# A mixture-of-experts block on one core: the last 128 tokens taken out of the dense expert products

## The reference, cut to what matters

```python
q = (xb @ w_q).reshape(p, 8, 2, 64)                    # 8 heads, two half queries
sc = einsum('phcd,hcnd->phcn', q, sub_keys)             # 128 scores for each half
top_s, top_i = top_k(sc, 16)
cand_s = top_s[:, :, 0, :, None] + top_s[:, :, 1, None, :]   # 16 x 16 sums
best_s, best_pos = top_k(cand_s.reshape(p, 8, 256), 16)
idx = take_along_axis(cand_i, best_pos, -1)             # first * 128 + second: one of 16384 experts
g = softmax(best_s)
act = gelu(einsum('phkd,pd->phk', expert_u[idx], xb))
out = einsum('phk,phkd->pd', g * act, expert_v[idx])    # 8 x 16 = 128 experts for each token
```

## Time and profile before

| | |
|---|---|
| time | 2292.05 us median of 3 runs (2291.0 to 2293.1) |
| span of the profiled execution | 2289.3 us |
| PE | 2225.7 us busy, 97% of the span |
| DVE, POOL, ACT | 1618.5, 1084.8 and 844.6 us busy (71%, 47%, 37%) |
| first product, 128 blocks | from 303.7 to 915 us of the span |
| second product, 128 blocks | from 922 to 1512 us |
| moved by DMA | 470.89 MB, 206 GB/s over the span |

### The profile page before, as it was taken

How to read it: one execution, slowest core, us unless ns; L and a number is a source line. 1 busy time by engine, 2 the same in 40 slices (tenths; PEclk the granted TensorE clock), 3 DMA queues, 4 the chain that set the end, 5 groups by cost and what they waited for, 6 DMA issues and landing times.

```text
span 2289.3 us, 30027 instructions
## 1 busy us (share of the span) xinstructions
PE 2225.7 (97%) x11272; PEld 2021.6 (88%) x11272; DVE 1618.5 (71%) x3044; ACT 844.6 (37%) x1317; POOL 1084.8 (47%) x695
## 2 busy tenths in 40 slices
PE   6999999999999999899999999999999999999998
PEld 3777889999999999899999999998877778888887
DVE  6774789998899763899898898747765565434323
ACT  4433433334333433333333333344355434323221
POOL 1334305878888787566566666354333331111100
PEclk9999999999999999899999999999999999999999
DMA  7647756668777885999999999633323333333332
GB/s 300 198 124 243 226 143 175 165 146 200 178 183 173 213 231 132 355 405 404 411 390 387 391 381 411 218 110 103 116 80 110 129 129 94 99 102 92 97 101 78
DMA packets 209848, 470.89 MB, mean 206 GB/s; under 512 B 50844, under 2 KB 106268, under 8 KB 208992
## 3 DMA queue, kind: packets, MB, share of 16 engines
q1 hardware_dynamic: 136552, 317.02, 42.3%
q0 software_dynamic: 73152, 151.94, 21.0%
HBM read 403.68 MB, written 61.28 MB: 203 GB/s over the span
## 4 chain that ended last, share of the span: by engine, by line
PE 58%; POOL 1%; DVE 1%; DMA 1%; issue 0%; ACT 0%; ACTq 0%
PE bank L571 15%; PE bank L572 15%; PE bank L575 15%; PE bank_stat L950 1%; PE bank_stat L951 1%; PE bank_stat L955 1%; PE bank_stat L572 1%; PE bank_stat L571 1%; PE bank_stat L575 1%; POOL expert_coefs L2533 1%; PE bank L995 1%; PE bank L982 1%; PE bank L980 1%; PE bank L723 1%; PE bank_stat L598 0%
## 5 line engine op out<-in xcount | busy, mean ns | idle before, releaser
L571 PE MATMUL bank<-h_lo,weights_hi 128*128 128x416 f32 (+1 forms) x2148 | 790.2, 368 | 8.4 <-DVE gates L2336 3.8
L572 PE MATMUL bank<-h_hi,weights_hi 128*128 128x416 f32 (+1 forms) x2148 | 788.4, 367 | 0.0
L1134 ACT ACTIVATE weights_hi<-weights_raw 128x1024 fp32r<-128x1024 f32 (+1 forms) x411 | 432.1, 1051 | 442.0 <-PE bank L575 318.4
L1658 DVE TENSOR_TENSOR weights_lo<-weights_raw,weights_hi 128x1024 fp32r<-128x1024 f32 x351 | 443.3, 1263 | 133.7 <-ACT weights_hi L1134 130.6
L2533 POOL DMA_INDIRECT expert_coefs<-square x256 | 447.8, 1749 | 156.0 <-issue 80.0
L575 PE MATMUL bank<-h_hi,weights_lo 128*128 128x416 f32 (+1 forms) x2148 | 479.6, 364 | 4.7 <-DVE weights_lo L1658 4.4
L571 PEld LDWEIGHTS bank<-h_lo,weights_hi 128*128 128x128 f32 x2148 | 407.8, 190 | 41.6 <-DVE gates L2336 3.9
L575 PEld LDWEIGHTS bank<-h_hi,weights_lo 128*128 128x128 f32 x2148 | 402.7, 188 | 37.5 <-DVE weights_lo L1658 7.1
L572 PEld LDWEIGHTS bank<-h_hi,weights_hi 128*128 128x128 f32 x2148 | 407.0, 189 | 31.0 <-issue 0.2
L2461 POOL TENSOR_TENSOR weights_lo<-weights_raw,weights_hi 128x1024 fp32r<-128x1024 f32 x60 | 147.0, 2455 | 222.6 <-ACT weights_hi L1134 222.6
L1345 ACT ACTIVATE hidden<-bank 128x416 f32<-128x416 f32 x128 | 66.3, 518 | 358.1 <-PE bank L575 336.5
(11 more groups left out here) (470 smaller groups left out, 3567.7 us busy)
## 6 DMA issues: line engine op xcount, KB each, us to landing
weights_raw<-in_expert_u SPq DMA_DIRECT2D x128, 512.0 KB
weights_raw<-in_expert_v SPq DMA_DIRECT2D x128, 512.0 KB
weight<-expert_coefs POOLq DMA_DIRECT2D x32, 832.0 KB
hidden_store<-hidden SPq DMA_DIRECT2D x28, 832.0 KB
hidden<-hidden_store POOLq DMA_DIRECT2D x28, 832.0 KB
ada_raw<-in_w_ada SPq DMA_DIRECT2D x34, 512.0 KB, 6.3
expert_coefs<-zeros SPq DMA_DIRECT2D x32, 512.0 KB, 6.3
weights_raw<-in_w_ffn_gate SPq DMA_DIRECT2D x22, 512.0 KB
```

Of the source, the lines that this page charges most:

```text
L571: M.matmul(bank[:, 0:width], hi[:, c:c + P], m_lo[k][:, 0:width], start=start and i == 0, stop=False)
L572: M.matmul(bank[:, 0:width], hi[:, c:c + P], m_hi[k][:, 0:width], start=False, stop=False)
L1134: S.activation(w_hi[n % SPLIT][:, 0:w], w_raw[n % RAW][:, 0:w], ACT.Copy).then_inc(*hi_done.inc(n))
L1658: V.tensor_tensor(w_lo[n % SPLIT][:, 0:w], w_raw[n % RAW][:, 0:w], w_hi[n % SPLIT][:, 0:w].bitcast(F32), ALU.subtract).then_inc(*lo_dve.in ...
```

## The change

The number of gathered tokens goes from 96 to 128, a whole token block, and `DT` from 416 to 384. A partition now holds one token and one indirect DMA one slot of all 128 tokens, 128 from `expert_u` and 128 from `expert_v`; the copies of `own` and `row_share` and the folding matmuls go. The tokens' own x comes straight into `own`, row buffers are six and lie over the scores of blocks already routed. Row steps begin at j = 91: 32 there, 12 beside the last eight first-product blocks (where DVE's `mix_tile` is now interleaved too, from the third on), 212 over the 120 slots. One token block is scattered (tb 0), two are placed by quads (tb 1 and 2, 64 quads). For a quad DVE makes both kinds of one-hot rows in one operation of 1024 elements, and ACT multiplies the weights in with eight copies of 128 elements; PE places one j later, DVE adds one later again. The second top 16 looks at 112 sums in place of 256 (a candidate needs (rank+1) products of at most 16, so 4 x 16 and 12 x 4 hold all), with five more small operations for the indices. The rotary table moves beside the last group of the second product, three operations to a block. POOL makes the low part of three more blocks.

```diff
-PICKED = 96
-BATCH = 32
+PICKED = P
 DT = T - PICKED
-ROWS = 5
-SCATTERED = 2
+ROWS = 6
+SCATTERED = 1
+WIDE = 4
+CANDIDATES = WIDE * TOPK + (TOPK - WIDE) * WIDE
...
-POOL_LOW = set(range(0, BLOCK_AT["expert_u", 2])) \
+POOL_LOW = set(range(0, BLOCK_AT["expert_u", 5])) \
...
+        own, row_sum = halves[0]
+        rows = [half for tb in range(1, TB) for half in halves[tb]]
...
+        ROWS_IN_U = 32
+        ROW_STEPS = {}
+        for q in range(ROWS_IN_U):
+            ROW_STEPS.setdefault(("u", 91 + 7 * q // 8), []).append(q)
+        ROWS_EARLY = ROWS_IN_U
+        for n in range(GROUP):
+            ROW_STEPS[0, "u", n] = list(range(ROWS_EARLY, ROWS_EARLY + 1 + (n >= HALF)))
+            ROWS_EARLY = ROW_STEPS[0, "u", n][-1] + 1
+        for q in range(ROWS_EARLY, 2 * HEADS * TOPK):
+            ROW_STEPS.setdefault(SLOTS[(q - ROWS_EARLY) * len(SLOTS) // (2 * HEADS * TOPK - ROWS_EARLY)], []).append(q)
...
+        ROUTED_AT = [[None] * HEADS + [0, 0, 1, 2, 3, 4, 5, 6, 6, 7],
+                     [8 + 7 * n // 6 for n in range(ROUTE_STEPS)],
+                     [29 + 7 * n // 4 for n in range(ROUTE_STEPS)],
+                     [60 + 7 * n // 4 for n in range(ROUTE_STEPS)]]
+        for tb, quad in in_order:
+            HOT_AT.setdefault(30 + 44 * (tb - SCATTERED) + 11 * quad // 8, []).append((tb, quad))
...
-                            for b in range(BATCHES):
-                                ins = M.matmul(held_bank(k)[:, DT + b * BATCH:DT + (b + 1) * BATCH], own[b][:, k * P:(k + 1) * P],
-                                               fold[:], start=True, stop=True)
+                            ins = M.matmul(held_bank(k)[:, DT:T], row_sum[:, k * P:(k + 1) * P], const("ident"), start=True, stop=True)
...
+            def weigh_hot(tb, quad):
+
+                S.wait_ge(*dve["hot", tb, quad])
+                if (tb, quad) in TWO_BEFORE:
+                    S.wait_ge(*pe["place", TWO_BEFORE[tb, quad]])
+                for t in range(4):
+                    at = slice(4 * quad + t, 4 * quad + t + 1)
+                    for part, w in enumerate((route_hi[tb % 2][:, at].bitcast(F32), route_lo[tb % 2][:, at])):
+                        S.activation(hot_weight[quad % N_HOT][:, t, part, :], hot[quad % N_HOT][:, 1, t, :].bitcast(F32), ACT.Copy, scale=w) \
...
-                V.tensor_tensor(hot[:], placed[:, 0, t0:t0 + 4].unsqueeze(2).broadcast_to([P, 4, P]),
...
-                        V.tensor_scalar(weights[:, t, part, :], const("iota"), placed[:, 1, t0 + t:t0 + t + 1],
-                                        w[:, t0 + t:t0 + t + 1], ALU.is_equal, ALU.mult) \
...
+                V.tensor_tensor(hot[quad % N_HOT][:], placed[:, 0:2, t0:t0 + 4].unsqueeze(3).broadcast_to([P, 2, 4, P]),
+                                const("iota").unsqueeze(1).unsqueeze(1).broadcast_to([P, 2, 4, P]), ALU.is_equal) \
...
                     for n in range(GROUP):
                         split_lo(BLOCK_AT["expert_u", (g + 1) * GROUP + n] + 2)
+                        if n >= 2:
+                            mix_tile(i, n - 2)
                         for q in ROW_STEPS.get((i, "u", n), ()):
                             row_step(q)
-                    for n in range(GROUP):
+                    for n in range(GROUP - 2, GROUP):
                         mix_tile(i, n)
...
+            for q in range(ROWS_IN_U + ROWS - 1):
+                load_rows(q)
             for tb in range(SCATTERED):
                 G.wait_ge(*scattered[tb][HEADS - 1, TOPK - 1])
             G.wait_ge(*stage_stored[0][DT // TOK - 2])
```

More of the change, by code:

```diff
@@ L812, in place @@
             def place(tb, quad):
-                M.wait_ge(*dve["hot", tb, quad])
-                hot, weights = one_hot[quad % N_HOT], hot_weight[quad % N_HOT]
+                M.wait_ge(*act["hot_weight", tb, quad])
+                tokens, weights = hot[quad % N_HOT][:, 0], hot_weight[quad % N_HOT]
                 for half in range(2):
@@ L817, in place @@
                     for t in range(2):
-                        ins = M.matmul(bank[:, 256 * t:256 * t + 256], hot[:, 2 * half + t, :],
+                        ins = M.matmul(bank[:, 256 * t:256 * t + 256], tokens[:, 2 * half + t, :],
                                        weights[:, 2 * half + t, :, :].rearrange("p h n -> p (h n)"), start=True, stop=True)
                     ins.then_inc(*pe.inc(("place", tb, quad, half)))
-                pe.also(("place", tb, quad), ("place", tb, quad, 1))
+                pe.also(("place", (tb, quad)), ("place", tb, quad, 1))
             for j in range(AHEAD * GROUP):
@@ L825, in tensor @@
                     turn_chosen(TURNED_AT[j])
-                for tb, quad in QUADS_AT.get(j, ()):
+                for tb, quad in HOT_AT.get(j - 1, ()):
                     place(tb, quad)
-                if j == 1:
+                if j == OWN_AT:
                     own_tokens()
@@ L1438, in scalar @@
                         if k == KD - 2:
+                            S.wait_ge(*dve["angle"])
+                            S.activation(table[:], table[:], ACT.Sin).then_inc(*act.inc("sine"))
                             load_sqrt("x2")
@@ L2073, in vector @@
                 split_lo(BLOCK_AT["expert_u", j] + 2)
-                if j >= TABLE_AT:
-                    for _ in range(2):
-                        next(turning, None)
+                for tb, quad in HOT_AT.get(j - 2, ()):
+                    placed_quad(tb, quad)
+                for q in ROW_STEPS.get(("u", j), ()):
+                    row_step(q)
             late = []
@@ L2150, in vector @@
                     if i == len(MIX_ORDER) - 1:
+                        for _ in range(3):
+                            next(turning, None)
                         V.wait_ge(*act["h3_hi", k])
```

258 lines of the change are left out of this document (101 added, 157 removed).

## The result

| | median, us | lowest to highest |
|---|---|---|
| before, same chip | 2292.4 | 2291.0 to 2293.1 (4 runs) |
| after | 2274.96 | 2270.6 to 2278.5 (4 runs) |

The ratio is 0.9936 [0.9913, 0.9958]: 17 us faster, where I had forecast 39. The profiled execution took 2276.32 us with a span of 2275.0, so span against span 14.3 us are gained. PE is busy for 2162.0 us (95%), DVE for 1650.9, ACT for 1005.6 and POOL for 953.5; 494.96 MB are moved.

The account below looks back on a forecast made before the run. PE sets the pace in both products, with DVE close behind in the first and transfers in the second. First product -26.5, between the products -11, second product -2: -39.5 us, from 2292 to 2253 us; range 2216 to 2280.

Parts of the forecast that it names:

- Narrower matmuls: Both products: a block of 24 matmuls takes 4.19 us, 0.33 less; 42 us per product if PE sets the pace.
- the rival of 2%: Both products: weight loads set 0.188 us a matmul, so the width gives nothing; about 2298 us, chance 2%.
- The place matmuls: First product: 24 more quads, 96 matmuls of 256 columns at 0.120 us, add 11.5 us to PE's path.
- Between the products: Join of the two products: PE's stop and low clock mostly go, a gain of 11 us.
- the 2 us of stops that I took: Join of the products: PE still loses 2 us, bounds 0 to 4, or 13 if nothing is hidden.
- the 1 us beside the last eight blocks: End of the first product: 13.6 MB of transfers take 33.5 us, just PE's eight blocks; 1 us added.
- Second product: Second product: transfers at 407 GB/s decide; groups 36.5 us for 36.2, +4 us over 14 groups; -2 us in all.
- the transfers keep up: Second product: groups run at PE's or DVE's pace, -28 us instead of +4; 2221 us, chance 15%.
- the second product gets slower than forecast: Second product: at 382 GB/s groups take 38.6 us, kernel 2283; 10% for 2270 to 2287, 8% for more.
- First product: First product: narrower blocks -42, place matmuls +11.5, waits +3, transfers in the last eight blocks +1; -26.5 us.
- DVE or ACT late in the first product: First product: runs of heavy steps at 92% load cost 10 to 25 us more; 2263 to 2278 us, chance 15%.
- The table's three DVE operations a block: Last group of the second product: about 2 us a block beside 4.2, with DVE otherwise at 2.6; +1 us.

Follow-up runs that it names:

- e4: Kernel after with every second gather of the second kind left out (61 of 128), DVE's arithmetic kept: 2261.22 us, one run.
- e5: Kernel after with most of DVE's arithmetic left out of every second row step from the 45th on, all gathers kept: 2275.12 us, one run.
- e3: Kernel after with DVE making the one-hot rows before its routing step in each j: 2263.96 us, 0.988 of the kernel before.
- e1: Kernel after with the rotary table back beside the first product and its sine moved earlier: 2260.11 us, 0.9874 of the kernel before.
- e11: As e10, but the routing steps dealt out more thinly, with quads and own x later: 2238.24 us, 0.9768 of the kernel before.
- e12: Kernel after with the edits of e1 and e3, nine POOL low parts and the first block's routing dealt later: 2244.78 us, 0.9797 of the kernel before.
- e10: As e12, but POOL makes five low parts at the start instead of nine: 2245.97 us, 0.9806 of the kernel before.

## Why the prediction was wrong

**Narrower matmuls: right.** 4.16 us a block for 4.19, and no floor from the weight loads; the rival of 2% is out. The place matmuls came as priced: eight blocks with about six quads take 36.2 us, without quads 33.3.

**Between the products: right.** The table has 17.7 us where the sum had 12.3. I had let the first group of the second product run at 36.5 us, and it took 34.4, with the transfers at 371 GB/s in it; and the 2 us of stops that I took, and the 1 us beside the last eight blocks (33.3 us), did not come.

**Second product: right, and for the stated reason.** 36.30 us a group for 36.5, 407 to 410 GB/s. That the width buys nothing there is shown by e4 and e5: less transfer quickens it, less DVE work does not. The exception is the group of blocks 240 to 247, which was to be 2.6 us shorter than before and is 2.2 longer. It takes 38.4 us at 323 GB/s, with one stop of 3.0 us for the product's high part, and 36.6 to 39.4 in every profile but e4's (35.8) whatever else is changed; why is open. The rivals in which the transfers keep up (15%) or the second product gets slower than forecast did not come.

**First product, "I take 3 us of waits more than now, since the heavy steps come in runs": the step that failed.** It weighed the work of each engine over many j and came to 92% for DVE. Two things were not in that. At the start DVE was at 97% before too, with a routing step and a low part to each block, so there was no slack for the narrower blocks to use: PE needs 16 x 4.16 = 66.6 us for the first sixteen and 3.5 for 32 other matmuls that stand there before and after, and took 84.2 (82.4 before, where it needed 75.8). The order made it one long stop that took the clock with it. And a place matmul hangs on a chain of three engines (one-hot rows on DVE, eight copies on ACT, PE one j later), so that not DVE's sum but the place of `make_hot` in its list decides; e3 changes only that and gains 12 us. In place of 3 us more, PE's stops in blocks 0 to 119 came to 22.3 us against 7.0 before, 15 more, with the lower clock behind the two longest on top. This was the rival "DVE or ACT late in the first product" (15%), with 10 to 25 us named; the waits for weighted rows came where it looked for them (544 to 701 us), the long one for `weights_lo` at 340 did not. ACT's work was never too much: the copies take 0.39 us by their records, above the 0.31 that I took as their most, but start 0.29 apart.

**"The table's three DVE operations a block [...] +1 us": the second step that failed.** It measured some 14 us (e1). I had put DVE "otherwise at 2.6" us a block, but its low part took 2.3 us beside POOL's additions in the kernel before already (row 1488.56), and with residual and `h_lo` that is 3.7. The table's 1.6 to 2.2 us came on top and pushed `h_lo` into POOL's operation (1.66 us, not 0.75), which makes 6.1 to 6.6 us a block for 4.16 to 4.45 of PE: DVE set the pace. And the sine, with its table load, was costed at nothing. Both halves are seen in e1: 5.9 us up to block 255, some 8.5 behind it; which part of the 8.5 is the sine, which the late `h_lo` and which the fallen clock was not separated.

**The size.** 12 us (order of the quads), 14 (table) and 6.5 (start, e11 against e12) make up the 33 us by which e11 stands under the kernel after (2271.5 - 2238.2). The two ran on different chips; by their ratios it is 38 us, within what the intervals leave. e11 is 15 us under my forecast, and faster than both kernels, 52 us under the one before. So the kernel after had given over half of that back. How much of the 52 us is the narrower product alone is not shown: the kernel before also lost 6.6 us in its first sixteen blocks, and it was never run with its own steps spread.

## What to carry to other kernels

A load of 92% over 100 us says nothing of the one instruction that another engine waits for: for each new hand-over, read in the list what stands ahead of it in the same step, and add that up. Look at the first and the last blocks of a loop by themselves, since they have the extra work; here the stops of 5 us and more there took TensorE's clock too. Before work is put on an engine that is "free", look in the trace at whether its operations get longer beside its neighbour's.

## What the runs showed of the hardware

**DVE operations with two inputs in SBUF stood while POOL's subtraction or addition ran.** A DVE `TENSOR_TENSOR` of 128 elements took 2.53 us in place of 0.28 when it started 0.01 us after a POOL one of 2.4 us, the next 2.34 in place of 0.26 (rows 315.63 and 318.20); `h_lo` took 0.75 us at 1490.60 with POOL idle at its start, and 2.33 at 1496.69 beside a POOL operation from 1496.12. A low part on POOL so costs DVE up to 2.2 us where it meets such an operation, and saves it 1.14; by e10 against e12, four of them were worth about 1.4 us together. The Trainium skill, page "SBUF — State Buffer", section "SBUF: two separate sides", has this as an exclusive lock: one of the two holds the shared ports for its whole instruction, and the other stands. The trace agrees: DVE's two operations end 0.1 to 0.2 us after POOL's two (318.16 and 320.54 against 318.0 and 320.4). An operation with one such input kept its time: beside POOL's low part of 298.19 to 300.59, DVE's two `MAX8` of 298.64 took 0.48 us, as elsewhere.

**The transfers held 407 GB/s over 470 us** (938 to 1409.6, share 1.02), between the 435 and the 358 of the Trainium skill's page "DMA: Bandwidth & Descriptors" (section Bandwidth); the second is not a limit for this lone core.

**Stops of PE of 5 to 12 us were followed by matmuls at half the rate** (2.93 us for eight in place of 1.55); after those of about 1 us in the kernel before and in e11 the window's clock stayed 1.00. In between both came: behind a stop of 1.8 us in e3 (694.6) the granted clock was 0.55 over the next 3 us, behind one of 3.0 us in the kernel after (1124.1) it was 1.00.
